# Rows of routed tokens fetched by indirect transfers and turned, instead of gathered with one-hot products

## The chip, the cores and the metric

The kernel is one program on one core of a Trainium2 chip. The metric is the device time of one execution in microseconds, the median of three runs. Other times come from one profiled execution.

## The reference

Two blocks of a model run one after the other on 512 tokens of 1024 elements, in float32. The first block has two mixing branches, then a hierarchical mixture of experts; the second has attention, a linear attention and a feed-forward part. Only the mixture of experts matters here:

```python
grp_logits = xt @ w_grp                                  # 4 groups
exp_logits = (xt @ w_exp).reshape(T, N_GROUPS, EXP_PER_GROUP)
sel_logits = take_along_axis(exp_logits, g_sel)          # the best group's 8 experts
top_l, top_e = lax.top_k(sel_logits, 2)                  # 2 experts for each token
...
def expert_block(args):
    xb, e = args
    return (jax.nn.silu(xb @ w1[e]) * (xb @ w3[e])) @ w2[e]
...
contrib = ybuf[dest] * w_s[:, None]
out = jax.ops.segment_sum(contrib, tok_s, num_segments=T)
```

There are 32 experts; `w1` and `w3` are 1024 x 512 and `w2` is 512 x 1024, 2 MiB each. 512 tokens with 2 experts each make 1024 rows.

## The kernel before

The experts are taken two at a time: 16 pairs, in 8 batches of two pairs. Each expert has 64 places (`SLOTS`), so that a pair fills the 128 partitions. A token's rank among those of its expert is its place. If an expert has more than 64 rows, further rounds follow (`r` is then not None); here the fullest expert has 55.

**Weights.** A ring of six buffers of 2 MiB (`ring[0]` to `ring[5]`) holds the weights of one pair: halves 0 and 1 are `w1`, 2 and 3 `w3`, 4 and 5 `w2`. SyncE (SP) loads half m of the next pair (L908) as soon as the products of this pair's half m are done (`half_used`). Pair 1's halves 0 and 1 have buffers of their own, `extra0` and `extra1` (L923, L926), so that the ring's halves 0 and 1 go to pair 2 at once.

**TensorE, in order, for each pair.** *up*: 64 products of the gathered rows `xgT` and the halves 0 to 3 (L3815). In odd pairs then the *gather* of the next batch (L3722): for 8 slices of 128 features, two parts of the rows (`xn_hi`, `xn_lo`) and 4 tiles of 128 tokens, one product of the rows with the one-hot table `sel`, 64 in all, with 256 columns each (the places of both pairs). Then the *turn* of `gated` (L3425), the *spread* of the pair before (16 products, L3761, added to `x` by VectorE), and *down*: 32 products with halves 4 and 5 (L3828).

**The other engines.** VectorE makes `sel` for the next batch with 16 comparisons and 16 comparisons with an add (`make_sel`, L2661, L2666), multiplies the gate (L2698), makes the one-hots of the spread (L2702), and adds the spreads to `x` (L2673). ScalarE copies the gathered banks into `xgT` (L1586) and the outputs out of PSUM (L1614). GpSimd has no work in this stage; its next instruction is a row scale of the stage after it (L1195).

**Before the experts.** The normalised rows `xn_at[1]` (tokens on partitions) are made by VectorE tile by tile (L2226), split into `xn_hi` and `xn_lo` (L2213), and turned for the router's logits. `pair(1)` gathers batch 1 and the first batches are written out; the batches 2 to 7 are gathered in a hardware loop (`pe.Fori(1, BATCHES - 1)`), `pair(m * 2 + 1)` gathering batch m + 1. After the experts come the end of the first block and all of the second.

Semaphores that the change touches: `sel_made` (one-hots ready), `rows_in` (four gathered banks of a batch written) and `rows_out` (a bank copied to `xgT`), `up_done` (a half's products done), `xn_lo_done` (a tile of `xn_lo` written).

Of the kernel before, what the change touches and what calls it, by code (L numbers as in the profile page):

```python
# [21 lines left out]
ALU = mybir.AluOpType  # L22
ACT = mybir.ActivationFunctionType
F32 = mybir.dt.float32
F32R = mybir.dt.float32r
I32 = mybir.dt.int32
# [3 lines left out]
P = 128  # L30
# [45 lines left out]
def two_blocks(nc, A, out):  # L76
    T, D = A["x"].shape[1:]
    NT, KT = T // P, D // P
# [17 lines left out]
    PAIRS = NE // 2  # L96
    ROUTED = NG + NE
    FAR = 4096
    FIRST_PLACE = -2 * ROUNDS * FAR
# [39 lines left out]


    gates_dram = nc.dram_tensor("branch_gates", [2 * KT, P, T], F32).ap()

    ctx = ExitStack()
    with ctx:
# [6 lines left out]
        def at(name, page, shape, dt=F32):  # L151
            return nc.alloc_sbuf_tensor_at(name, shape, dt, offset=base + int(page * PAGE))

        def sem(name):
            return ctx.enter_context(nc.semaphore(name))
# [46 lines left out]
        slot_gate, slot_token = slot_tables[:, 0, :], slot_tables[:, 1:1 + NT, :]  # L202
# [16 lines left out]
        w_lo = [at(f"w_lo{s}", 45 + 4 * s, [P, 4, 512], F32R) for s in range(2)]  # L219
        F = 53  # L220

        xn_at = {1: 41, 2: F + 36, 6: F + 40}
        xn_at = {n: at(f"xn_{n}", page, [P, NT, D]) for n, page in xn_at.items()}
        xn_at.update({n: xn_at[2] for n in (3, 4, 5)})
        gain = at("gain", F + 48, [P, D])
# [46 lines left out]

        EXTRA = 2
        extra = (at("extra0", 29, [P, 8, 512]), [at(f"extra1{q}", page, [P, 4, 512]) for q, page in enumerate((37, 49))])
        pair_both = at("pair_both", 16, [P, 2 * NT, 2, PAIRS])
        route_f = at("route_f", F + 50, [P, KT, ROUTED])
        routed_T = at("routed_T", 13, [P, KT, T])
# [161 lines left out]
        n_xn, n_tp, n_hi, n_lo = sem("n_xn"), sem("n_tp"), sem("n_hi"), sem("n_lo")  # L439
        first_by_dve, x_hi, x_lo = sem("first_by_dve"), sem("x_hi"), sem("x_lo")  # L440
        gain_in, gain_2_in, gain_4_in = sem("gain_in"), sem("gain_2_in"), sem("gain_4_in")
        const_pool, const_dve, params_in = sem("const_pool"), sem("const_dve"), sem("params_in")
# [3 lines left out]
        wsp_masked = sem("wsp_masked")  # L446
# [21 lines left out]
        xn_hi_done, xn_lo_done = sem("xn_hi_done"), sem("xn_lo_done")  # L468
# [3 lines left out]
        sel_made, selT_out = sem("sel_made"), sem("selT_out")  # L472

        rows_in, rows_out = sem("rows_in"), sem("rows_out")
        up_done, down_done = sem("up_done"), sem("down_done")
# [4 lines left out]
        extra_in = sem("extra_in")  # L480
# [28 lines left out]

        b_added = gates_stored  # L510
        quo_summed, quo_out = first_in[1], first_in[2]
        row_highs, row_lows = far_in
        rows_again = first_in[3]
        out_stored = sem("out_stored")

        block = ctx.enter_context(nc.Block())
# [13 lines left out]
        def rows_count(n, t):  # L530

            return n * NT + t + 1
# [239 lines left out]
            return i if r is None else i + r * PAIRS  # L772

        BATCHES = PAIRS // 2

        def batch_number(m, r):

            return m if r is None else m + r * BATCHES

# [4 lines left out]
        def gather_bank(b, first):  # L784

            return ((mb[0], mb[1], gb[2], gb[3]) if first else (mb[0], mb[1], mb[0], mb[1]))[b]
# [16 lines left out]
        def _(sp):  # L803
# [98 lines left out]
            def half_of(m, pair):  # L902

                return A[("w1", "w3", "w2")[m // 2]][ds(pair * 2 + m % 2, 1)]
# [14 lines left out]
            sp.wait_ge(w_lo_done, split_count(g_out.chunk1 - 1))  # L919
            for m in range(3, 6):  # L920
                load_half(m, 0)
            extra_0 = extra[0][:, :, :].rearrange("p k n -> p (k n)")
            sp.dma_start(extra_0, half_of(0, 1).rearrange("o p q k n -> p (o q k n)")).then_inc(extra_in, 16)  # L923
            sp.wait_ge(pe_tiles, 4 * g_out.chunk1)
            for q in range(2):
                sp.dma_start(extra[1][q][:, :, :].rearrange("p k n -> p (k n)"),  # L926
                             half_of(1, 1)[:, :, q, :, :].rearrange("o p k n -> p (o k n)")).then_inc(extra_in, 16)


            for m in range(EXTRA):  # L930
# [177 lines left out]
        def _(pool):  # L1108
            own = Chain(pool, pool_own)
# [80 lines left out]
            own.settle()  # L1190
            pool.sem_inc(r_pool, 1)


            pool.wait_ge(n_sd, rows_count(2, NT - 1))
            own.did(pool.tensor_scalar(ssq[:, :], ssq[:, :], EPS, None, ALU.add))  # L1195
# [30 lines left out]
            for n in range(SB_STEPS):  # L1226
                t, s = n % NT, n % 2
# [964 lines left out]
        def _(dve):  # L2192
            own = Chain(dve, dve_own)
# [481 lines left out]
            def experts_dve(r):  # L2675
# [42 lines left out]
                def pair(i, first=False, following=None, turned_late=False):  # L2718
                    n = pair_number(i, r)
                    if following is not None:  # L2720
                        make_sel(following, batch_number(following, r))
                    gate_up_product(n)
                    if not turned_late:
                        gatedT_copy(n)
                    if first:
                        dve.wait_ge(tabled, 1 if r is None else r + 1)
                        dve.tensor_copy(slot_tables[:, 0:2, :], gb[1][:, 0:2 * PAIRS]  # L2727
                                        .rearrange("p (v i) -> p v i", i=PAIRS)).then_inc(valued, 1)
                        dve.wait_ge(valued, 1 if r is None else r * NT + 1)
                        for t in range(1, NT):  # L2730
                            dve.tensor_scalar(slot_token[:, t, :], slot_token[:, 0, :], -float(t * P), None, ALU.add)\
                                .then_inc(valued, 1)
                        dve.wait_ge(valued, NT if r is None else r * NT + NT)
                    else:

                        if not isinstance(n, int) or n > 1:
                            dve.wait_ge(moe_added, n * 8 - 8)
                        for u in range(2 * NT):
                            if u == 3 and turned_late:
                                gatedT_copy(n)  # L2740
                            add_spread(n - 1, u, u // 2, u % 2, spread_bank(u))
                    make_selT(i)
                    outputs_low(i, n)
# [26 lines left out]

                pair(0, first=True, following=1)
                pair(1)
                with dve.Fori(1, BATCHES - 1) as m:
                    pair(m * 2, following=m + 1, turned_late=True)
                    pair(m * 2 + 1)
                pair(PAIRS - 2, turned_late=True)
                last_pair()
# [233 lines left out]
            for n in range(SB_STEPS):  # L3011
                h, t = divmod(n, NT)
# [364 lines left out]
        def _(pe):  # L3377
# [46 lines left out]
            def turn(dst, src, rows=P):  # L3424
                return pe.transpose(dst, src, ident[0:rows, 0:rows])  # L3425
# [290 lines left out]
            def experts_pe(r):  # L3716
# [28 lines left out]
                def gather(b):  # L3745

                    pe.wait_ge(sel_made, b * 16 + 16)
                    for k in range(KT):
# [5 lines left out]
                        if k % 2:  # L3754
                            ins.then_inc(rows_in, 1)

                def spread(n, t, half, bank):

                    half = slice(half * 512, (half + 1) * 512)
                    for part in (y_hi_sb, y_lo_sb):  # L3760
                        ins = pe.matmul(bank[:, :], selT[:, t * P:(t + 1) * P], part[:, half],  # L3761
                                        start=(part is y_hi_sb), stop=(part is y_lo_sb))
                    ins.then_inc(spread_done, 1)
# [65 lines left out]
                                     ring[4 + k // 2][:, 4 * q + 2 * (k % 2) + nh, :], start=(k == 0),  # L3829
                                     stop=(k == 3), skip_group_check=True)  # L3830

                def pair(i, first=False, ahead=False, odd=0, following=None):
                    n = pair_number(i, r)
                    up(i, first, ahead, odd)
                    if first:
                        gate_table()
                    if following is not None:
                        gather(batch_number(following, r))
                    if first or odd:
                        turn_gated(n)  # L3840
                    if first:
                        pe.wait_ge(valued, 1 if r is None else r * NT + 1)
                    else:
                        output_cut(n - 1)
                        for u in range(2 * NT):
                            if odd and u in (3, 4):
                                pe.wait_ge(rows_out, n * 2 + (u + 2))
                            elif u == 5 and not odd:
                                turn_gated(n)
                            elif u == 7:  # L3850
                                pe.wait_ge(moe_added, n * 8 + (3 - 8))
                            spread(n - 1, u // 2, u % 2, spread_bank(u))
                        pe.wait_ge(moe_added, n * 8 - 6)
                    pe.wait_ge(gatedT_out, n + 1)
                    for kh in range(2):
                        half_in(n, 4 + kh, ahead)
                        for k in (2 * kh, 2 * kh + 1):
                            for nh in range(2):
                                for q in range(2):
                                    ins = down_matmul(n, k, nh, q)  # L3860
                                if k == 3:
                                    ins.then_inc(down_done, 1)
                        if kh == 0:
                            ins.then_inc(down_done, 1)
# [40 lines left out]
                pair(1, ahead=r is None, odd=1, following=1)  # L3905
                with pe.Fori(1, BATCHES - 1) as m:
                    pair(m * 2)
                    pair(m * 2 + 1, odd=1, following=m + 1)
                pair(PAIRS - 2)
                last_pair()  # L3910

# [152 lines left out]
            for n in range(SB_STEPS):  # L4064
                h, t = divmod(n, NT)
# [255 lines left out]
```

## Time and profile before

| | us |
|---|---|
| median of 3 runs | 1666.09 |
| lowest, highest | 1663.88, 1666.44 |
| span of the profiled execution | 1661.6 |
| experts' stage in it | about 346 to 809 |

The span goes from the first to the last instruction. The profiled execution's own time outside its span is not given apart; the median of the runs is 4.5 us above the span. TensorE's granted clock is at its full level nearly all the time (mean 0.999). Matmuls are pipelined, so the duration of one is longer than its distance to the next; distances are read from the chain in order of time. The profile has two views of the transfers: stretches with the busy share of the 16 DMA engines and GB/s, and for each line that issues them the time from issue to landing.

### The profile page before, as it was taken

Reading aid. Unit: us, or ns where it says so; the run is one execution under the profiler, and the core shown is the slowest. Engines: PE = TensorE matmul, PEld = TensorE weight load, DVE = VectorE, ACT = ScalarE, POOL = GpSimd, SP = SyncE. Lnnn points to the kernel's source line nnn. Section 1 sums busy time; section 2 is a strip of 40 time slices with the busy share of each in tenths; the row PEclk is TensorE's granted clock in tenths of the full one; section 3 lists DMA queues with packets and bytes.
Section 4 is the critical chain, followed back from the end, with each engine's and each line's share of the span. In section 5 each row is a group of like instructions: output and inputs, shape, how many; then the busy total and the mean of one; then the engine's idle time right before and its main releaser. Section 6 shows DMA issues by size and latency. Waiting matters only on the chain.

```text
span 1661.6 us, 25424 instructions
## 1 busy us (share of the span) xinstructions
PE 1649.0 (99%) x10378; PEld 1246.5 (75%) x10378; DVE 1042.9 (63%) x1371; ACT 715.6 (43%) x906; POOL 109.6 (7%) x168
## 2 busy tenths in 40 slices
PE   9999999999999999999999999999999999999998
PEld 7899998864535545453688877788888889889986
DVE  6989777453243334323668746567675577878887
ACT  6576552411101101111456533344642367757775
POOL 4000100000000000000011022210000001000000
PEclk9999999999999999999999999999999999999999
DMA  7232224958999999999441232123353249667864
GB/s 279 66 114 76 102 81 183 400 208 341 427 428 429 429 428 429 427 429 428 185 177 33 100 102 77 51 77 129 114 179 110 92 146 255 158 182 226 202 144 121
DMA packets 92209, 355.65 MB, mean 214 GB/s; under 512 B 7936, under 2 KB 7952, under 8 KB 79824
## 3 DMA queue, kind: packets, MB, share of 16 engines
q1 hardware_dynamic: 79776, 328.04, 50.8%
q0 software_dynamic: 12336, 26.23, 8.0%
q8 instruction: 71, 1.16, 0.3%
q14 instruction: 26, 0.21, 0.0%
HBM read 347.97 MB, written 6.29 MB: 213 GB/s over the span
## 4 chain that ended last, share of the span: by engine, by line
PE 97%; DVE 1%; DMA 1%; ACT 1%; issue 0%; POOL 0%; ACTq 0%; POOLq 0%; DVEq 0%
PE bank L3400 33%; PE bank L3815 13%; PE bank L4267 9%; PE bank L3563 9%; PE bank L3828 7%; PE bank L4242 6%; PE bank L3722 4%; PE bank L3761 4%; PE bank L3998 2%; PE bank L3425 2%; PE bank L3446 1%; DMA stage<-in_w_ff 1%; PE bank L3923 1%; PE bank L4028 1%; PE bank L4051 1%; PE bank L4098 1%
## 5 line engine op out<-in xcount | busy, mean ns | idle before, releaser
L3815 PE MATMUL bank<-ring,xgT 128*64 128x512 f32 x992 | 216.1, 592 | 0.6 <-ACT xgT L1586 0.6
L3400 PE MATMUL bank<-act_hi,w_hi 128*128 128x512 f32 x544 | 215.3, 396 | 0.0
L3400 PE MATMUL bank<-act_hi,w_lo 128*128 128x512 f32 x544 | 212.0, 390 | 0.0
L3400 PE MATMUL bank<-act_lo,w_hi 128*128 128x512 f32 x544 | 211.8, 389 | 0.0
L3815 PEld LDWEIGHTS bank<-ring,xgT 128*64 128x64 f32 x992 | 71.8, 137 | 141.0 <-issue 140.0
L2198 DVE TENSOR_TENSOR w_lo<-w_stage,w_hi 128x2048 fp32r<-128x2048 f32 x51 | 116.9, 2292 | 66.6 <-ACT w_hi L1291 64.9
L1291 ACT ACTIVATE w_hi<-w_stage 128x2048 fp32r<-128x2048 f32 x50 | 96.0, 1921 | 144.8 <-PE bank L3400 133.4
L4267 PE MATMUL bank<-down,part_hi 128*128 128x512 f32 x448 | 138.2, 390 | 0.2 <-issue 0.2
L3400 PEld LDWEIGHTS bank<-act_hi,w_hi 128*128 128x128 f32 x544 | 102.2, 188 | 23.2 <-issue 2.8
L3400 PEld LDWEIGHTS bank<-act_hi,w_lo 128*128 128x128 f32 x544 | 102.1, 188 | 21.7
L1614 ACT ACTIVATE y_hi_sb<-bank,slot_tables 128x512 fp32r<-128x512 f32 x32 | 22.0, 687 | 222.0 <-PE bank L3828 220.7
L3400 PEld LDWEIGHTS bank<-act_lo,w_hi 128*128 128x128 f32 x544 | 102.2, 188 | 20.3
L3828 PE MATMUL bank<-ring,gatedT 128*64 128x512 f32 x512 | 113.4, 595 | 0.9 <-DVE slot_tables L2727 0.9
L2698 DVE TENSOR_TENSOR gated<-gated,bank 128x512 f32<-128x512 f32 x16 | 11.0, 688 | 161.6 <-PE bank L3815 161.6
L4267 PEld LDWEIGHTS bank<-down,part_hi 128*128 128x128 f32 x448 | 83.8, 188 | 18.3 <-issue 1.0
L3828 PEld LDWEIGHTS bank<-ring,gatedT 128*64 128x64 f32 x512 | 35.3, 137 | 70.5 <-issue 66.8
L4267 PE MATMUL bank<-down,part_lo 128*128 128x512 f32 x224 | 87.2, 389 | 0.0
L2673 DVE TENSOR_TENSOR x_tm<-x_tm,bank 128x512 f32<-128x512 f32 x128 | 78.5, 679 | 0.3 <-PE bank L3761 0.3
L2714 DVE SCALAR_TENSOR_TENSOR y_lo_sb<-bank,slot_tables,y_hi_sb 128x512 fp32r<-128x512 f32 x32 | 23.5, 750 | 70.2 <-ACT y_hi_sb L1614 69.9
L4242 PE MATMUL bank<-act_hi,slot_hi 128*128 128x256 f32 x224 | 63.5, 283 | 0.1
L3563 PE MATMUL bank<-row_hi,slot_hi 128*128 128x256 f32 x224 | 63.5, 284 | 0.0
L4242 PE MATMUL bank<-act_lo,slot_hi 128*128 128x256 f32 x224 | 63.4, 283 | 0.0
(587 smaller groups left out, 3778.8 us busy)
## 6 DMA issues: line engine op xcount, KB each, us to landing
ring<-in_w SPq DMA_DIRECT2D x93, 2048.0 KB, 16.3
w_stage<-in_w_in SPq DMA_DIRECT2D x39, 1024.0 KB, 5.0
w_stage<-in_w_ff SPq DMA_DIRECT2D x19, 1024.0 KB, 5.8
b_sum<-in_w_ff POOLq DMA_DIRECT2D x12, 1024.0 KB, 12.0
w_stage<-in_w_out SPq DMA_DIRECT2D x8, 1024.0 KB, 5.0
b_one<-in_w_ff SPq DMA_DIRECT2D x6, 1024.0 KB, 7.5
stage<-in_w_ff SPq DMA_DIRECT2D x5, 1024.0 KB, 6.2
x_tm<-in_x SPq DMA_DIRECT2D x8, 512.0 KB, 9.3
```

Source lines behind the costliest of these rows:

```text
L1291: act.activation(w_hi[s][:, 0:ktiles, :], w_stage[s][:, 0:ktiles, :], ACT.Copy)\
L2198: dve.tensor_tensor(w_lo[s][:, 0:ktiles, :], w_stage[s][:, 0:ktiles, :], w_hi[s][:, 0:ktiles, :].bitcast(F32), ALU.subtract).then_inc(w_lo ...
L2673: dve.tensor_tensor(xt, xt, bank[:, :], ALU.add).then_inc(moe_added, 1)
L3400: ins = pe.matmul(banks[j][:, :], left, right, start=(kc == 0 and k == 0 and n_pass == 0), stop=(kc == g.chunks - 1 and k == g.ktiles - 1 ...
L3425: return pe.transpose(dst, src, ident[0:rows, 0:rows])
L3563: ins = pe.matmul(bank_of[:, 256 * f:256 * f + 256], left[:, k, cols], right[:, k, :], start=(n in (0, 1, 3) and f == 0 and k == 0 and n_p ...
L3722: return pe.matmul(bank[:, (k % 2) * 2 * P:(k % 2 + 1) * 2 * P], part[:, t, k * P:(k + 1) * P], sel[:, t, :], start=start, stop=(part is x ...
L3761: ins = pe.matmul(bank[:, :], selT[:, t * P:(t + 1) * P], part[:, half], start=(part is y_hi_sb), stop=(part is y_lo_sb))
L3815: ins = pe.matmul(dst[mine, :], xgT[:, 4 * kh + k, slots], up_weights(2 * w + kh, q, k, ahead), start=(kh == 0 and k == 0), stop=(kh == 1 ...
L3828: return pe.matmul(gb[1 + nh][mine, :], gatedT[:, k, mine], ring[4 + k // 2][:, 4 * q + 2 * (k % 2) + nh, :], start=(k == 0), stop=(k == 3 ...
L4242: ins = pe.matmul(bank[:, 256 * f:256 * f + 256], left[:, k, cols], right[:, k, :], start=(n in (0, 1, 3) and f == 0 and k == 0 and n_pass ...
L4267: ins = pe.matmul(part_bank[h][n][j][:, :], left[:, ka, cols], right[:, k, :], start=(part_first[n] and kc == 0 and k == 0 and n_pass == 0 ...
```

## The change

The rows `xn_at[1]` are stored to a DRAM tensor `routed_rows`. For batches 2 to 7 (`FETCHED = 2`) GpSimd clears a buffer `slot_rows` and issues two indirect transfers per batch, one for each pair, that fetch the row of each place by its token number (`slot_row`; a place without a token has a number beyond the bound and is skipped). TensorE turns these rows, 16 turns of 128 x 128, into the banks that the one-hot products filled before. Batches 0 and 1 stay as they are. VectorE no longer makes `sel` for batches 2 to 7. The buffer `xn_at[1]` lies on other pages, and the load of `extra0`, which shares these pages now, is issued after the rows are stored and `xn_lo` is made.

```diff
-        xn_at = {1: 41, 2: F + 36, 6: F + 40}
+        xn_at = {1: 29, 2: F + 36, 6: F + 40}
+        slot_row = at("slot_row", 15, [P, PAIRS], I32)
+        slot_rows = at("slot_rows", 37, [P, 2, D])
...
 @ SyncE
-            extra_0 = extra[0][:, :, :].rearrange("p k n -> p (k n)")
-            sp.dma_start(extra_0, half_of(0, 1).rearrange("o p q k n -> p (o q k n)")).then_inc(extra_in, 16)
             sp.wait_ge(pe_tiles, 4 * g_out.chunk1)
             for q in range(2):
                 sp.dma_start(extra[1][q][:, :, :].rearrange("p k n -> p (k n)"),
                              half_of(1, 1)[:, :, q, :, :].rearrange("o p k n -> p (o k n)")).then_inc(extra_in, 16)
+            for t in range(NT):
+                sp.wait_ge(n_xn, rows_count(1, t))
+                sp.dma_start(rows_dram[t * P:(t + 1) * P, :], xn_at[1][:, t, :]).then_inc(rows_stored, 16)
+            sp.wait_ge(xn_lo_done, NT)
+            sp.wait_ge(rows_stored, STORED)
+            sp.dma_start(extra[0][:, :, :].rearrange("p k n -> p (k n)"),
+                         half_of(0, 1).rearrange("o p q k n -> p (o q k n)")).then_inc(extra_in, 16)
 @ GpSimd
+            pool.wait_ge(rows_stored, STORED)
+            pool.wait_ge(row_listed, LISTED)
+            pool.wait_ge(up_done, 4 + EXTRA)
+            for b in range(FETCHED, BATCHES):
+                if b > FETCHED:
+                    pool.wait_ge(rows_in, 4 * b)
+                own.did(pool.memset(slot_rows[:, :, :], 0.0))
+                own.settle()
+                for q in range(2):
+                    i = 2 * b + q
+                    pool.indirect_dma_start(slot_rows[:, q, :], None, rows_dram[:, :],
+                                            bass.IndirectOffsetOnAxis(ap=slot_row[:, i:i + 1], axis=0),
+                                            bounds_check=T - 1, oob_is_err=False).then_inc(rows_fetched, 16)
 @ VectorE
+                        if r is None:
+                            dve.tensor_scalar(slot_row[:, :], slot_token[:, 0, :], -float(FIRST_PLACE), None, ALU.add)\
+                                .then_inc(row_listed, 1)
...
-                    pair(m * 2, following=m + 1, turned_late=True)
+                    pair(m * 2, following=None if r is None else m + 1, turned_late=True)
 @ TensorE
+                def turn_slots(m):
+
+                    b = batch_number(m, r)
+                    pe.wait_ge(rows_fetched, m * 32 + (NONE_FETCHED - 32 * (FETCHED - 1)))
+                    for k in range(KT):
+                        if k in (4, 6):
+                            pe.wait_ge(rows_out, b * 4 + (k // 2 - 1))
+                        for q in range(2):
+                            first = (k % 2) * 2 * P + q * P
+                            ins = turn(gather_bank(k // 2, False)[:, first:first + P],
+                                       slot_rows[:, q, k * P:(k + 1) * P])
+                        if k % 2:
+                            ins.then_inc(rows_in, 1)
...
-                    if following is not None:
+                    if fetched:
+                        turn_slots(following)
+                    elif following is not None:
                         gather(batch_number(following, r))
...
-                    pair(m * 2 + 1, odd=1, following=m + 1)
+                    pair(m * 2 + 1, odd=1, following=m + 1, fetched=r is None)
```

## Rows read from the trace of the kernel before

**Rows 1.** The page: busy time by engine, and the last chain by engine.
```profile
PE 1649.0 (99%) x10378; PEld 1246.5 (75%) x10378; DVE 1042.9 (63%) x1371; ACT 715.6 (43%) x906; POOL 109.6 (7%) x168
...
PE 97%; DVE 1%; DMA 1%; ACT 1%; issue 0%; POOL 0%; ACTq 0%; POOLq 0%; DVEq 0%
```

**Rows 2.** Chain in order of time: start us, us, what; 360 to 860.
```profile
375.68 13.73 PE bank L3815 x64
...
433.46 13.73 PE bank L3815 x64
447.19 7.87 PE bank L3722 x64
455.06 0.44 PE bank L3425 x4
...
491.26 13.73 PE bank L3815 x64
...
790.56 0.03 issue
790.59 3.65 PE bank L3815 x16
```

**Rows 3.** Stretches: length; busy us by engine; TensorE's clock, DMA share, GB/s.
```profile
400.00:405.00 5.00, 5.00 (x24) 2.12 (x25) 3.99 (x10) 0.00 (x0) 0.00 (x0) 1.00 0.00 0
433.50:491.30 57.80, 57.80 (x298) 27.97 (x296) 20.66 (x48) 6.33 (x11) 0.00 (x0) 1.00 1.01 428
722.50:780.30 57.80, 57.80 (x298) 27.97 (x296) 16.89 (x33) 6.33 (x10) 0.00 (x0) 1.00 1.01 428
365.00:370.00 5.00, 4.12 (x30) 2.76 (x30) 2.68 (x10) 0.00 (x0) 0.00 (x0) 1.00 1.01 433
780.00:800.00 20.00, 19.97 (x94) 8.31 (x92) 10.31 (x14) 4.34 (x6) 0.00 (x0) 1.00 1.01 410
335.00:350.00 15.00, 14.04 (x109) 11.76 (x108) 13.76 (x57) 1.40 (x4) 0.00 (x0) 1.00 0.01 3
```

**Rows 4.** Ring loads by issue time, with us to landing; then TensorE's wait.
```profile
L908 SPq DMA_DIRECT2D ring<-in_w x1: 333/333/333, 433.5 to 433.5; - x1
DMA to landing us min/median/max: 14.4/14.4/14.4
...
L908 SPq DMA_DIRECT2D ring<-in_w x1: 333/333/333, 722.5 to 722.5; - x1
DMA to landing us min/median/max: 19.1/19.1/19.1
...
L908 SPq DMA_DIRECT2D ring<-in_w x1: 328/328/328, 768.9 to 768.9; - x1
DMA to landing us min/median/max: 21.6/21.6/21.6
...
PEld bank L3815 <- DMA ring<-in_w: 0.9, 1, 0.9
```

**Rows 5.** Single lines: ns min/median/max, first and last start.
```profile
L1586 ACT ACTIVATE xgT<-bank x28: 597/597/597, 391.5 to 744.1; 128x512 f32<-128x512 f32 x28
...
L1177 POOL MEMSET attT<- x1: 1813/1813/1813, 172.0 to 172.0; 128x2048 f32 x1
```

**Rows 6.** Timelines of SyncE's queue and of VectorE: start us, us.
```profile
350.53 25.52 SPq L908 DMA_DIRECT2D ring<-in_w  x6
382.58 0.33 SPq L937 DMA_DIRECT2D pT<-in_p  x1
...
337.78 1.22 DVE L2213 TENSOR_TENSOR xn_lo<-xn,xn_hi 128x1024 fp32r<-128x1024 f32 x1
```

**Rows 7.** Queues: packets, MB, share of 16 engines; 1050 to 1250, then whole span.
```profile
q0 software_dynamic: 1280, 4.20, 5.4%
...
q1 hardware_dynamic: 79776, 328.04, 50.8%
q0 software_dynamic: 12336, 26.23, 8.0%
```

More of the change, by code:

```diff
@@ L141, in two_blocks @@
     gates_dram = nc.dram_tensor("branch_gates", [2 * KT, P, T], F32).ap()
+    rows_dram = nc.dram_tensor("routed_rows", [T, D], F32).ap()
     ctx = ExitStack()
@@ L511, in two_blocks @@
         quo_summed, quo_out = first_in[1], first_in[2]
+        row_listed, LISTED = wsp_masked, 2
+        rows_fetched, NONE_FETCHED = params_in, 16 * 9
         row_highs, row_lows = far_in
         rows_again = first_in[3]
+        rows_stored, STORED = rows_again, 16 + 2 * 16 * NT
         out_stored = sem("out_stored")
@@ L774, in two_blocks @@
         BATCHES = PAIRS // 2
+        FETCHED = 2
         def batch_number(m, r):
@@ L2772, in experts_dve @@
                 pair(1)
+                if r is None:
+                    dve.wait_ge(sel_made, 16 * FETCHED)
+                    dve.sem_inc(sel_made, 16 * (BATCHES - FETCHED))
                 with dve.Fori(1, BATCHES - 1) as m:
-                    pair(m * 2, following=m + 1, turned_late=True)
+                    pair(m * 2, following=None if r is None else m + 1, turned_late=True)
                     pair(m * 2 + 1)
@@ L3830, in down_matmul, with pair @@
                                      stop=(k == 3), skip_group_check=True)
-                def pair(i, first=False, ahead=False, odd=0, following=None):
+                def pair(i, first=False, ahead=False, odd=0, following=None, fetched=False):
                     n = pair_number(i, r)
```

## The prediction

> **What bounds the kernel now.** I read the page first. TensorE is busy 99% of the span and 97% of the chain that ended last [rows 1], so a cut of TensorE work looks like a cut of the time. The share is an average over stages, so I went to the experts' stage: first to the chain of waits in order of time [rows 2]. There, one batch of two expert pairs repeats every 57.80 us (433.46 to 491.26) without a gap: an up product of 13.73 us, the gather of 7.87 us, a turn of 0.44 us, eight spreads, the down product, then the second pair without a gather. The reader is to see that TensorE paces this stage and that the edited gather is in its pace.
>
> The table of stretches gives the other half [rows 3]: in the same 57.80 us the DMA engines are 1.01 busy and move 428 GB/s, and still are in 722.5 to 780.3. One batch of pairs needs 12 loads of 2 MiB, 25.17 MB, and at 428 GB/s these take 58.8 us. The DMA engines are asked for one microsecond more per batch than TensorE allows. The loads' own rows confirm it [rows 4]: the load issued at 433.5 lands 14.4 us later, the same load of the batch five periods on, issued at 722.5 (289.0 us later), after 19.1 us. The lag grew 4.7 us in 5 periods, 0.94 us each, so 12 loads take 57.80 + 0.94 = 58.74 us. What hides this is the lead that the ring had at the start. It is used up at the very end: the load issued at 768.9 lands at 790.5, and the chain shows TensorE at 790.56 with 0.03 us between two pieces just there [rows 2]; the waits list has one wait of 0.9 us of TensorE's weight loads for a ring load, the only one [rows 4]. So the two limits meet at 790.5. The stream of loads is unbroken back to the empty stretch 400 to 405 [rows 3].
>
> **The change, part by part.** *TensorE.* Six gathers (batches 2 to 7) of 7.87 us go [rows 2]. In place of 64 products come 16 turns. Four turns of `gated` take 0.44 us, so 16 take 1.8 us; turns 9 and 13 wait for ScalarE to empty a bank, 0.60 us a piece [rows 5]: 0.44 us for the first four, then four evacuations of which two must be done before the last four turns, with some 0.2 us of handing over, make about 2.3 us. Bounds: 1.8 and, one evacuation after another, 4 us. TensorE saves 5.6 us per batch, 33 us in six (23 to 36). A batch then costs it 52.2 us of work.
>
> That saving can't be cashed. After the change the DMA engines still need 58.74 us for the loads of each batch, and no load becomes smaller or goes away. A faster TensorE frees ring buffers earlier, but the queue has not been empty since 405, so an earlier issue only waits longer. The last ring loads land when all bytes ahead of them have been moved; the last up product, spreads, down product and everything after follow from that landing by the same TensorE work as before. TensorE's 33 us turn into waits for ring loads. From this part the end moves by 0 us.
>
> *The added traffic.* Each of the six batches has two fetches of up to 128 rows of 4 KB. Places beyond an expert's rows hold an index beyond the bound and are to be skipped. Counted with the reference's routing on its inputs, 1024 rows are spread over 32 experts, 21 to 55 each; batch 2 has 109, batches 3 to 7 have 119, 104, 106, 167 and 155, together 651. The first fetch waits for the second half of pair 1, which `pT` waits for too (issued at 382.6) [rows 6]; it falls ahead of the idle 400 to 405 [rows 3], and its 109 rows (0.45 MB, 1.0 us) are absorbed there. The other five wait for the batch before to be turned, the first after about 450, and all run inside the unbroken stream. 651 x 4096 bytes are 2.67 MB: 6.2 us at the stream's 428 GB/s, 6.5 us at the 410 GB/s of 780 to 800 where smaller transfers are mixed in [rows 3]. They displace ring loads byte for byte, so the end moves by that.
>
> Is a fetched row as cheap as a byte of the ring? No row of before shows an indirect transfer. Nearest are the direct transfers from GpSimd's queue: the gate stores, 4.20 MB for 5.4% of 16 engines over 200 us, 389 GB/s while busy; the page's other queue has 328.04 MB for 50.8% of 1661.6 us, 389 GB/s too; all of GpSimd's traffic, mostly accumulating, 26.23 MB for 8.0%, 197 GB/s [rows 7]. So a plain transfer costs alike from both queues, and at the worst row 651 rows would take 13.5 us. Were empty places moved as well, 5 x 256 rows are 5.24 MB, 12.2 us at 428 and 26.6 us at 197. A second unknown is how rows are divided among the engines: experts fill only the first half of their places, and if that left half of the engines idle, the loaded ones would need twice as long, 13 us. Below, an even split gives 6.2. I take 8 us: nearest to the even split, a little above it because experts with 55 and 47 rows of 64 cannot split evenly and ten more transfers bring their completions. Could it be below nothing? Only if a second queue raised the total rate; that is a rival.
>
> The Trainium skill (DMA: Bandwidth & Descriptors, The descriptor swizzle) gives a map in which the first 32 places of each 64 lie on eight engines, four each. By it the most loaded engine would carry 52 of the rows and the delay would be 8.0 us as an estimate; no row here shows the map.
>
> *The store and the moved load.* Four stores of 512 KB and the load of `extra0` now come after the halves of `extra1`. The same 2 MB of `extra0` left the stretch before 335, and 2 MB of stores took its place. DMA engines are idle (0.01) from 335 to 350 [rows 3]. The load now also waits for the last `xn_lo` (337.8 + 1.2 = 339.0) [rows 6] and needs 4.9 us for its bytes and at most as much again on idle engines: landed by 349, read by pair 1 from 375.7 [rows 2], cost 0. What it delays on SP's queue is the first reload of the ring, issued at 350.5 [rows 6]: 11 us in hand, cost 0 (0 to 2; were the stores' completions late by 10 us, the idle 400 to 405 would take it up).
>
> *VectorE* loses the one-hots of six batches, 20.66 - 16.89 = 3.8 us a batch; it is busy 20.66 of 57.80 us, so 0 [rows 3]. *ScalarE* copies the same banks: 0. *GpSimd* is idle there; a clear of `slot_rows` is the size of one that took 1.81 us [rows 5]; behind its waits stands only the row scale of the next stage. A fetch must be in place a batch later, about 50 us; with clear, two issues, a queue of 16 to 25 us it needs some 30. Cost 0. `xn_at[1]` on other pages changes no wait.
>
> Sum: 0 + 8 + 0 = 8 us. The profiled span is 1661.6 us, so 1669.6; the median of the three runs is 1666.1, 4.5 us more (what lies around the span), so 1674.
>
> **Rivals.** (a) *Added bytes on a saturated stream, as above*: +8, range +5 to +14; chance 0.80. (b) *The other side: TensorE's saving is cashed.* The mechanism would be that 428 GB/s is what the one queue reaches and not what the engines can; rows fetched by another queue then ride beside it, and faster release lets more through. Single stretches reach 433 [rows 3]. It decides from the point where 390 us of stream shrink by 3.3 us more than the fetches cost, that is 10 us, 439 GB/s. Fully cashed it gives 1666.1 - 33 = 1633. Against it: 1.01 busy and a growing lag at any depth of the queue. Chance 0.07, mostly near 1660. The Trainium skill (DMA: Bandwidth & Descriptors, Issuing engines are not separate DMA queues) says that transfers of all issuing engines run on the same 16; by that the second queue adds nothing. (c) *Dear rows*: accumulating price or empty places moved: +13 to +27, 1680 to 1692; 0.05. (d) *A fetch comes late*: GpSimd needs more than 50 us per batch. At 60 us, TensorE waits 10 us in each of five batches, 1716; 0.02. (e) *The clock falls*: TensorE now waits. Its waits are short, since a load lands every 4.9 us and a half takes 3.43 us (a quarter of 13.73), and with 4.12 of 5 us busy it kept 1.00 in 365 to 370 [rows 3]. At 1.2 GHz a half would take 6.9 us and a batch over 100, some +40 us each; 0.01. The Trainium skill (TensorE: Matmul & The Clock Gate, HAM oscillation) tells of a kernel whose waits for data brought the half clock back each time; by it this would be the outcome if the waits were longer than its bursts. (f) *Nothing*: hidden or halved cost, below 3.3 us; 0.05.
>
> **From these to the numbers.** A change of 0.2% (3.3 us) is about what these runs can tell from none. Slower: (a), (c), (d), (e), 0.88; allowing for a mistake in the reading I give 0.85. Same 0.06. Faster 0.09. The predicted time is that of (a), 1674. The range holds (a) whole, 1671 to 1680, and reaches to the side of (f) and the start of (c): 1667 to 1682.
>
> **What the profile after would show.** If right: no pieces of the gather's line in the loop, turns instead; the same 428 GB/s and 1.01; TensorE no longer 99% busy but waiting for ring loads by name, 35 to 45 us in all; ring loads' lag level at 20 to 27 us (four to five loads in the queue), not growing; GpSimd's queue up by 3.1 MB; the last pair's half 3 landing about 8 us later than 790.5; `extra0` issued near 339. Wrong if the throughput rises above 435 GB/s, if TensorE waits for `slot_rows`, or if that half lands earlier than 790.5.

## The result and the profile after

The changed kernel takes 1673.36 us (median of 4 runs, 1671.48 to 1674.12), the kernel before 1666.17 (4 runs): a ratio of 1.0044 with a 95% interval of 1.0031 to 1.0056, which is 5 to 9 us. It is slower by 7.2 us; the forecast was 8 us and 1674.

The lines of the profile's page for the changed kernel: span, busy time, transfer queues, the last chain, and GpSimd's transfers.

```profile
span 1671.4 us, 24640 instructions
...
PE 1621.7 (97%) x10090; PEld 1209.9 (72%) x10090; DVE 1020.0 (61%) x1276; ACT 714.9 (43%) x906; POOL 133.0 (8%) x186
...
q1 hardware_dynamic: 80352, 330.14, 51.2%
q0 software_dynamic: 14064, 29.35, 8.5%
...
PE 81%; DMA 17%; DVE 1%; ACT 0%; issue 0%; SPq 0%; DVEq 0%; ACTq 0%
```

TensorE is busy 27 us less than in [rows 1], and yet the span is longer: 17% of the chain is now transfers of the ring. GpSimd's queue moves 3.12 MB more than in [rows 7], the 760 rows of the six batches.

These are stretches of the changed kernel, with the columns of [rows 3]:

```profile
335.00:350.00 15.00, 14.04 (x109) 12.00 (x110) 13.74 (x57) 1.40 (x4) 0.00 (x0) 1.00 0.63 244
395.00:400.00 5.00, 5.00 (x35) 4.62 (x35) 2.02 (x4) 1.20 (x2) 0.00 (x0) 1.00 0.98 412
400.00:405.00 5.00, 5.00 (x24) 2.19 (x24) 4.24 (x10) 0.00 (x0) 0.00 (x0) 1.00 0.06 20
405.00:410.00 5.00, 5.00 (x26) 1.72 (x24) 1.27 (x2) 1.37 (x2) 0.00 (x0) 1.00 0.80 279
433.50:491.30 57.80, 57.55 (x276) 23.83 (x274) 18.28 (x34) 7.06 (x12) 3.81 (x3) 1.00 1.01 427
450.00:780.00 330.00, 298.11 (x1387) 123.08 (x1387) 98.13 (x186) 33.07 (x55) 18.98 (x15) 1.00 1.01 427
```

From 450 to 780 the throughput is what it was (427 GB/s, 1.01 busy; 428 before), with another kind of bytes in it. TensorE stands still for 32 of 330 us, at full clock. The chain in order of time says for what; it is to be read against [rows 2].

```profile
408.62 13.73 PE bank L3862 x64
...
773.38 0.02 issue
773.40 25.62 DMA ring<-in_w
799.02 0.04 issue
799.06 3.65 PE bank L3862 x16
802.72 2.52 PE bank L3808 x10
```

Where the one-hot kernel ran on without a gap, the chain now goes through the load of the last pair's half 3: issued at 773.4, landed 25.6 us later, at 799.0. The same half landed at 790.5 before. To take out what varies between profiles ahead of the stage, I use one measure from here on: from the start of pair 2's up product to the start of the last pair's products with half 3. It is 790.59 - 408.37 = 382.2 us before (408.37 is the start of that piece in its chain) and 799.06 - 408.62 = 390.4 after: 8.2 us more. Each value comes from one profile; where two runs should agree, they do within 0.2 us (e1 and the kernel before, e2 and the changed kernel, e6 and e7 below).

The fetches by their line, with the time from issue to landing:

```profile
L1217 POOL DMA_INDIRECT slot_rows<-routed_rows,slot_row x12: 997/1002/1123, 385.6 to 689.3; - x12
DMA to landing us min/median/max: 10.3/12.8/15.4
```

The queues in 450 to 780, where all fetches of batches 3 to 7 lie (packets, MB, share of the engines):

```profile
q1 hardware_dynamic: 9501, 138.32, 98.6%
q0 software_dynamic: 1440, 2.67, 2.1%
```

2.67 MB are the 651 counted rows exactly; rows beyond the bound are not moved. A fetch is in place 15 us after its issue. The fetch of batch 3, issued at 452.5 and 453.8, is turned from about 502 on, 33 us after it landed; later batches have some 38 us.

### The profile page after: what moved, and what is told of

Its sections match the earlier page's. It is cut to its first block, busy times and chain, and to the rows that moved or that the text cites. A ratio compares the mean times of both kernels' runs of the same rounds, so it can differ in the third digit from the quotient of the medians.

```text
span 1671.4 us, 24640 instructions
## 1 busy us (share of the span) xinstructions
PE 1621.7 (97%) x10090; PEld 1209.9 (72%) x10090; DVE 1020.0 (61%) x1276; ACT 714.9 (43%) x906; POOL 133.0 (8%) x186
## 4 chain that ended last, share of the span: by engine, by line
PE 81%; DMA 17%; DVE 1%; ACT 0%; issue 0%; SPq 0%; DVEq 0%; ACTq 0%
PE bank L3433 33%; DMA ring<-in_w 17%; PE bank L4316 9%; PE bank L3596 8%; PE bank L4291 8%; PE bank L3862 7%; PE bank L4047 2%; PE bank L3875 2%; PE bank L3458 2%; PE bank L3479 1%; PE bank L3808 1%; PE bank L3755 1%; PE bank L4077 1%; PE bank L4100 1%; PE bank L4147 1%; PE bank L3972 1%
## 5 line engine op out<-in xcount | busy, mean ns | idle before, releaser
L3862 PE MATMUL bank<-ring,xgT 128*64 128x512 f32 x992 | 222.7, 595 | 34.9 <-DMA ring<-in_w 34.3
## 6 DMA issues: line engine op xcount, KB each, us to landing
b_sum<-in_w_ff POOLq DMA_DIRECT2D x12, 1024.0 KB, 10.9
```

Source lines behind the costliest of these rows:

```text
L3862: ins = pe.matmul(dst[mine, :], xgT[:, 4 * kh + k, slots], up_weights(2 * w + kh, q, k, ahead), start=(kh == 0 and k == 0), stop=(kh == 1 ...
```

## The experiments

The ratio of each run is taken to runs of the kernel before on the same chip. "Late" is the measure above less 382.2 us. The diffs show the main lines of each edit, "..." marks what is left out, and comments in them are mine.

| run | us (median) | ratio to before (interval) | measure, us | late, us |
|---|---|---|---|---|
| changed kernel | 1673.36 | 1.0044 (1.0031 to 1.0056) | 390.4 | 8.2 |
| e1 no transfers | 1666.29 | 1.0003 (0.9994 to 1.0012) | 382.2 | 0.0 |
| e2 one-hot gathers, fetches beside them | 1673.67 | 1.0046 (1.0032 to 1.0059) | 390.3 | 8.1 |
| e3 two more buffers | 1672.50 | 1.0041 (1.0027 to 1.0054) | see the text | |
| e4 all rows skipped | 1667.26 | 1.0008 (0.9999 to 1.0017) | 383.1 | 0.9 |
| e5 places 0 to 31 | 1671.91 | 1.0038 (1.0025 to 1.0052) | 388.7 | 6.5 |
| e6 places 0 to 63 | 1679.15 | 1.0079 (1.0065 to 1.0092) | 394.9 | 12.7 |
| e7 all places | 1679.56 | 1.0082 (1.0068 to 1.0096) | 394.8 | 12.5 |
| e8 before, light loads | 1665.29 | 0.9996 (0.9986 to 1.0005) | | |
| e9 changed, light loads | 1633.20 | 0.9804 (0.9788 to 0.9821) | | |
| e10 two more buffers, order of use | 1671.65 | 1.0031 (1.0019 to 1.0044) | 386.1 | 3.9 |
| e11 eight buffers in turn | 1667.82 | 1.0013 (1.0004 to 1.0022) | 383.5 | 1.3 |
| e12 eight buffers, no transfers | 1661.39 | 0.9967 (0.9958 to 0.9977) | 376.7 | -5.6 |

**Is it the fetches?** e1 takes the transfers away and leaves everything else; e4 issues them and moves nothing; e2 does them beside the old gathers.

```diff
 @ e1
-                    pool.indirect_dma_start(slot_rows[:, q, :], ...).then_inc(rows_fetched, 16)
+                    pool.sem_inc(row_listed, 1)
...
-                    pe.wait_ge(rows_fetched, m * 32 + (NONE_FETCHED - 32 * (FETCHED - 1)))
+                    pe.wait_ge(row_listed, m * 2 + (LISTED - 2 * (FETCHED - 1)))
 @ e2
-                    pair(m * 2, following=None if r is None else m + 1, turned_late=True)
+                    pair(m * 2, following=m + 1, turned_late=True)
...
-                    pair(m * 2 + 1, odd=1, following=m + 1, fetched=r is None)
+                    pair(m * 2 + 1, odd=1, following=m + 1)
```

> The changed kernel without its twelve indirect transfers: GpSimd clears the buffer and signals, TensorE turns the cleared rows, the store and the moved load stay. It leaves out the routed rows of batches 2 to 7. Theory of the stream (the DMA engines set the end, TensorE's saving is worth nothing, the fetches are the whole loss): 1666, within 1.5 us of the kernel before, TensorE waiting 30 to 37 us for ring loads. Rival that TensorE's saving is cashed once the fetches are gone: about 1633. Rival that the loss comes from the store, the moved load or the turns: stays near 1673.

> The changed kernel with its fetches, but the rows of batches 2 to 7 gathered with one-hot products as before; the fetched rows are not used. Nothing of the output is left out. Theory of the stream: as slow as the changed kernel, 1673 to 1674, because the loads and fetches of a batch need about 60 us and the one-hot kernel's TensorE 57.8 us. Rival that TensorE's waits for fetched and turned rows make the loss: 1666. Rival that both limits add up: above 1680.

> The changed kernel with a list in which every row number lies beyond the bound (1024 and up): twelve indirect transfers are issued and move no row. It leaves out the routed rows of batches 2 to 7. If a skipped row costs nothing and a transfer nearly nothing: as without transfers, 1666 to 1667. If the 8.3 us by which the last half landed later hold 2 us for ten transfers beside 6.2 us for 651 rows: 1668. If skipped rows cost as much as fetched ones: 1674 or more.

e1 came out as the kernel before in both the time (1.0003) and the measure (382.2): the fetches are the whole loss, and 33 us less TensorE work are worth nothing. TensorE's freed time is there as waits for loads, at a throughput of 428 GB/s. The next lines are e1's two sums of that kind in the waits list of 440 to 830 (us in total, times, longest), and its queue in 450 to 780:

```profile
PEld bank L3860 <- DMA ring<-in_w: 38.5, 24, 2.1
PE bank L3860 <- DMA ring<-in_w: 27.2, 26, 1.3
```

```profile
q1 hardware_dynamic: 9693, 141.25, 100.6%
```

e2 is the mirror of it: all of TensorE's old work and the fetches are as slow as the changed kernel (8.1 us late), so what TensorE saves does not matter on this side either. e4 is 0.9 us late: ten transfers that move nothing cost the stream 0.1 us each by the measure; the medians alone (1.0008, interval from 0.9999) do not tell that from nothing. A finer reading supports it: from one wait for a load to the next one, six loads later, 29.4 us pass in e1's chain, and 29.5 to 29.6 in e4's where two transfers lie between.

**Does TensorE's saving exist?** In e8 (the kernel before) and e9 (the changed kernel) the loads of pairs 3 to 14 bring half the bytes.

```diff
-                    load_half(m, i + 1)
+                    sp.dma_start(ring[m][:, 0:4, :].rearrange("p k n -> p (k n)"),
+                                 half_of(m, i + 1)[:, :, 0, :, :].rearrange("o p k n -> p (o k n)")).then_inc(ring_in[m], 16)
```

> The kernel before with half of the bytes in the loads of pairs 3 to 14: only the first expert's half of each buffer is loaded; it leaves out the second expert's weights there. TensorE's work is the same. Theory: TensorE paced this kernel to the edge, so 1666 (0 to 1 us less). If hidden waits for loads cost it more: well below.

> The changed kernel with the same loads of half the bytes for pairs 3 to 14; it leaves out the second expert's weights there. Theory: with the stream out of the way TensorE's saving of about 5.6 us in each of six batches shows: 1633, 33 us under the kernel before with light loads. Rival that the turns cost as much as the gathers, or that TensorE waits for the fetched rows: near 1666.

It does: 1665.29 - 1633.20 = 32.1 us. The one-hot kernel does not gain from lighter loads (0.9996), so TensorE paced it all through the stage. In e9's chain one batch takes 485.80 - 433.46 = 52.3 us, in place of 57.8:

```profile
433.46 13.73 PE bank L3863 x64
447.19 0.60 PE bank L3459 x4
447.79 0.02 issue
447.81 0.61 ACT xgT L1614
448.42 0.04 issue
448.46 1.58 PE bank L3459 x12
450.05 3.66 PE bank L3809 x16
...
485.80 13.73 PE bank L3863 x64
```

Between up product and spreads lie 2.86 us: the 16 turns, the turn of `gated`, and one wait for ScalarE (four of the turns run during that wait and so are not in the chain). Before there were 7.87 + 0.44 us [rows 2].

**What does a row cost?** In e5 to e7 the list of rows is 0 to 127 and the bound cuts it, so that places 0 to 31, 0 to 63 or all are filled in each of the ten transfers.

```diff
+            own.did(pool.iota(slot_row[:, :], pattern=[[0, PAIRS]], base=0, channel_multiplier=1))
+            own.settle()
...
-                                            bounds_check=T - 1, oob_is_err=False).then_inc(rows_fetched, 16)
+                                            bounds_check=31, oob_is_err=False).then_inc(rows_fetched, 16)     # 63, 127; e4: base=1024, bound 511
```

> The changed kernel with row number p for place p and the bound at 31: each indirect transfer fetches 32 rows, to places 0 to 31; ten transfers in the stream, 320 rows, 1.31 MB. It leaves out the routed rows of batches 2 to 7. 4096 bytes at a sixteenth of 428 GB/s take 0.153 us. Rows dealt evenly over 16 engines: 3.1 us over the kernel without transfers (1669). The first 32 places on eight engines, four each: 6.1 us (1672). Eight neighbouring places to one engine: four engines carry all, 12.2 us (1678).

> As the run with 32, bound at 63: 64 rows to places 0 to 63, 640 rows in the stream, 2.62 MB, nearly the bytes of the true lists. It leaves out the routed rows of batches 2 to 7. Even: 6.1 us (1672), as the changed kernel or a little less. Half of the engines carry eight rows each: 12.2 us (1678), clearly over the changed kernel with the same bytes.

> As the run with 32, bound at 127: all 128 places, 1280 rows in the stream, 5.24 MB. It leaves out the routed rows of batches 2 to 7. By bytes 12.2 us (1678) in every theory of the split; if the most loaded engine counts it equals the run with 64 rows, if bytes count it is 6.1 us over it. A cost per transfer would come on top in all three.

The queue of the transfers in 450 to 780 (packets, MB, share), one line each for e5, e6 and e7:

```profile
q0 software_dynamic: 1440, 1.32, 1.2%
```

```profile
q0 software_dynamic: 1440, 2.62, 2.1%
```

```profile
q0 software_dynamic: 1440, 5.24, 3.9%
```

The bytes double from run to run; the delay goes 6.5, 12.7, 12.5 us. Bytes in total do not decide. 64 rows in places 0 to 63 cost as much as 128 rows in all places, and the first 32 cost half of that. That fits a split in which places 0 to 63 lie on half of the engines, and 0 to 31 on the same half with four rows each. A row of 4096 bytes takes 0.153 us at a sixteenth of 428 GB/s, an estimate, which gives 6.1 and 12.2 us. The runs rule out rows dealt evenly (3.1 and 6.1) and eight neighbouring places to an engine (12.2 for the first 32); another split with the same largest load would fit as well. The Trainium skill (DMA: Bandwidth & Descriptors, The descriptor swizzle) gives this split for a plain transfer to 128 partitions. These three runs agree with it for the indirect one.

The changed kernel's own trace shows the same with the true lists. These are the pieces of its chain that are waits for loads, from 532 to 711; each load waited for is six loads after the one of the line above:

```profile
532.86 25.63 DMA ring<-in_w
562.22 26.99 DMA ring<-in_w
592.96 25.62 DMA ring<-in_w
622.32 27.58 DMA ring<-in_w
653.64 25.64 DMA ring<-in_w
683.01 27.90 DMA ring<-in_w
```

Start and length added give the landings: 558.5, 589.2, 618.6, 649.9, 679.3, 710.9. Six loads take 29.4 us where no fetch lies between, and 30.7, 31.3 and 31.6 us with the fetches of batches 5, 6 and 7. These fetches cost 1.4, 2.0 and 2.3 us. Batch 7 has fewer rows than batch 6 (155 against 167) and costs more. By the split above the reference's routing puts 8, 13 and 16 rows on the most loaded engine in them, 1.2, 2.0 and 2.4 us as an estimate; by bytes, batch 7 would be the cheaper one of the two (1.5 against 1.6 us).

**Where else could time come from?** The DMA engines idle between 395 and 410 (the stretches above: 0.1 + 4.7 + 1.0 = 5.8 us), because the pages for further loads are missing. From 398 on the split rows (`xn_hi`, `xn_lo`) are not needed any more. e3 puts their pages to use as two more buffers, for halves 0 and 1 of odd pairs from pair 3 on; e10 is e3 with the loads issued in the order of use; e11 uses all eight buffers in turn; e12 is e11 without the transfers.

```diff
 @ e3
+        wide = [at(f"wide{m}", page, [P, 8, 512]) for m, page in enumerate((21, 41))]
...
+                        half_used(j * 2 + odd, m)
+                        if m < 2:
+                            load_next(m, j * 2 + (odd + 2), odd)     # pair after next, ring or wide by parity
 @ e10: load_next(0) and load_next(1) behind half 5 of the next pair
 @ e11
+        eight = ring[0:4] + wide + ring[4:6]
...
+            with sp.Fori(0, 3) as j:
+                for s in range(6, 30):
+                    n, m = j * 4 + (s // 6 + 2), s % 6
+                    slot_used(n, m)      # the buffer's load of eight loads ago
+                    load_slot(s, n)      # into eight[s % 8]
```

> The changed kernel with two more ring buffers for halves 0 and 1, on the pages of the split rows, which are free after batch 1 is gathered: pair 3's halves are loaded at about 397 in place of 412, and from there even and odd pairs have buffers of their own. Further rounds (none is run with these inputs) are not provided for. Theory of the stream: the DMA engines' idle time between 398 and 406, about 7 us, is filled, so the whole stream ends 7 us earlier: 1666. If the stream is not what sets the end from 406 on, but bursts of the fetches that single waits feel: 1673, or between.

> The kernel with two more ring buffers again, but in the loop the loads of halves 0 and 1 of the pair after next are issued behind the next pair's half 5, so that loads stand in the queue in the order of their use. Further rounds are not provided for. If the run without this order gained only 0.9 us because two early halves stood ahead of the ones needed sooner: the idle time left is some 3 us less than in the changed kernel, so 1670. If filling the idle time is worth nothing: 1673.

> The changed kernel with a ring of eight buffers used in turn, in the order of use, from pair 2's half 4 on (the six buffers and the pages of the split rows). Further rounds are not provided for. The changed kernel's DMA engines are idle for 5.8 us between 395 and 410; theory of the stream: all of it is filled, every later load lands that much earlier, 1667.5. If the end is not set by the stream: 1673. Below 1666 would need more than the idle time gives.

> The ring of eight buffers without the indirect transfers (the cleared rows are turned). It leaves out the routed rows of batches 2 to 7, and further rounds. Theory of the stream: both effects add, 1666 - 5.8 - 0, 1660; here TensorE's saving lets the filled idle time show below the kernel before. If the one-hot kernel's time were a floor of TensorE or of something else: 1666.

e3's forecast missed: it was 1666, and 1672.5 were measured. Its DMA engines are busy through the empty stretch, as meant. The same table shows something else: at three places, of which the lower rows show one, TensorE's clock fell to half for a few us after a wait.

```profile
400.00:410.00 10.00, 10.00 (x47) 4.31 (x47) 5.62 (x13) 1.13 (x2) 0.00 (x0) 1.00 1.02 428
...
554.00:556.00 2.00, 1.28 (x6) 0.14 (x2) 0.00 (x0) 0.60 (x1) 0.00 (x0) 1.00 1.04 442
556.00:558.00 2.00, 0.11 (x2) 0.11 (x4) 0.00 (x0) 0.00 (x0) 0.00 (x0) 1.00 0.96 410
558.00:560.00 2.00, 2.00 (x6) 0.59 (x8) 0.00 (x0) 0.00 (x0) 0.00 (x0) 0.51 1.02 434
560.00:562.00 2.00, 2.00 (x8) 0.62 (x6) 0.00 (x0) 0.00 (x0) 0.00 (x0) 0.64 0.98 418
```

TensorE stood for 2.6 us (0.72 + 1.89) and then took 5.38 us for a piece with one half that takes 3.68 otherwise. The three losses of 1.7 us add up to nearly what e3 lacks, so they are a rival explanation. The landings in e3's chain answer it: 30.7 us pass from 557.9 to 588.6, across the first loss, as in the changed kernel with its full clock (558.5 to 589.2), and 29.4 us from 649.3 to 678.7, across the second (29.4 from 649.9 to 679.3). So these two losses are hidden behind the stream. The third lies where TensorE's waits move on to another half and cannot be compared like this. The chain at the end shows where the gain went:

```profile
748.31 25.63 DMA ring<-in_w
773.94 0.04 issue
773.98 3.65 PE bank L3883 x16
777.64 2.50 PE bank L3824 x10
...
781.98 7.02 PE bank L3896 x32
789.00 13.73 PE bank L3883 x64
802.73 2.50 PE bank L3824 x10
```

Halves 0 and 1 of the pair after next stood in the queue ahead of halves that were needed sooner. So the last half waited for is one of the pair before the last, landed at 773.94, with 28.8 us of TensorE work from it to the last pair's spreads at 802.73, against 802.72 in the changed kernel (from the start of pair 2's up product, at 409.42 and 408.62, it is 0.8 us less). The last pair's own up product (789.00, 13.73 us) runs without a wait: the end of the stream had stopped being what TensorE waits for. In order of use (e10, forecast 1670) the delay falls from 8.2 to 3.9 us by the measure. That profile is of the fastest of its six runs (1668.17). Four of the six lie at 1671.6 to 1672.2, and the median, 1671.65, is not clear of e3's by the intervals; so e10 shows the direction, not the size. e11 leaves 1.3 us of 8.2, and a time of 1667.82 (forecast 1667.5), 1.9 us over the kernel before. That is 6.9 us back by the measure where the idle time held 5.8; what the last 1.1 us are is open. Its stretches show the idle time filled:

```profile
395.00:400.00 5.00, 5.00 (x39) 4.78 (x38) 1.15 (x2) 1.36 (x3) 0.00 (x0) 1.00 1.00 421
400.00:405.00 5.00, 5.00 (x23) 2.60 (x23) 5.00 (x12) 0.00 (x0) 0.00 (x0) 1.00 1.00 419
405.00:410.00 5.00, 5.00 (x26) 1.72 (x24) 0.62 (x2) 1.07 (x2) 0.00 (x0) 1.00 1.02 436
```

e12 (1661.39, forecast 1660) is below the kernel before: filled idle time shows as soon as TensorE has time in hand and the fetches are gone. No run that computes the whole output is faster than the kernel before. Eight buffers with the one-hot gathers were not run; by e8, where the lighter loads gained nothing, I expect nothing from them.

## Why the prediction was right

- *The stream sets the end*: shown by e1 (nothing gained without fetches), e2 (nothing lost with the old gathers) and e12 (gained only by moving the stream forward). Two limits met in the kernel before; taking one away leaves the other. The forecast 58.74 us for the 12 loads of a batch are 2 x 29.4 = 58.7 us between the landings of e1.
- *TensorE saves 5.6 us a batch, 33 in all*: 5.5 a batch in e9's chain (57.8 - 52.3), 32.1 in all. Hidden until e9.
- *The fetches cost 8 us*: 8.2 by the measure, 7.2 in the medians, whose interval is 5 to 9. The size was in part luck. "They displace ring loads byte for byte" did not hold: e5 to e7 and the single batches go by the most loaded engine, and the even price of 6.2 us by bytes would have been too low. The 8 was a choice between 6.2 and 13 with a reason, uneven experts and the transfers' completions, that pointed the right way but gave no number. Worked out from the runs, the true lists put 52 rows on one engine, 8.0 us as an estimate; with e4's 0.9 us for ten transfers it is 8.9 at most, where 8.2 were seen.
- *Skipped rows are not moved*: the queue moved 2.67 MB, the bytes of the 651 rows, and 0.01 MB in e4. The accumulating queue's price (13.5 us) did not apply.
- *The store and the moved load cost 0*: e1, which keeps both, is as fast as the kernel before, but the reason given was not the whole one. The load of `extra0` waited for the stores to land, not for the last `xn_lo`: SyncE waited 10.9 us for `routed_rows`, the stores took 9.6 to 11.2 us. It was issued at 340.5, forecast 339.0, and landed in 7.8 us, before the first reload.
- *The lag is level at 20 to 27 us*: the loads' medians are 25.1 to 25.6 in each 50 us from 500 to 750, after 22.1 in 450 to 500; single loads up to 27.9. *TensorE waits 35 to 45 us*: 31.9 us idle in 450 to 780 and 3.6 in the 20 us after.
- *Rivals*: the cashed saving needed a higher throughput; it stayed at 427. No wait for fetched rows appears, and a fetch landed 10.3 to 15.4 us after its issue, sooner than the queue of 16 to 25 us that was allowed for it. The prediction took TensorE's waits as short; single ones reached 2.8 us. In the changed kernel the clock stayed full (1.00) through them. Other runs show that the clock rival was not empty: e3 lost the clock at three places, e6 at three and e10 at one.

## What to carry to other kernels

When an engine and the transfers are both near 100%, compute both demands for one round of the loop and follow the lag of a load over the rounds: a growing lag says that the transfers are the lower limit and only a lead hides it. Then work taken from the engine is worth nothing, and what is added to the transfers is paid in full; what pays is idle time of the transfers ahead of the stream, filled in the order of use. What e3 lacked against e11 is the order, as I read the chains; e10, the run made to test it, shows only the direction. A fetch of rows costs by its most loaded DMA engine, so where the rows land matters as much as how many they are.

## What the runs showed of the hardware

- An indirect transfer to 128 places does not cost by its bytes: filling the first 32 places delayed the stream 6.5 us over ten transfers, the first 64 12.7, all 128 12.5. In the changed kernel 155 rows cost 2.3 us and 167 rows 2.0.
- Ten indirect transfers that skip every row cost the stream 0.9 us. Each takes GpSimd 1.0 us to issue, whether it moves 0, 32, 64 or 128 rows (993 to 1123 ns in the changed kernel and e4 to e7).
- In e3 TensorE's clock fell to half (0.51) after the engine had stood for 2.6 us, and was full again from 562 on. In e6 it fell at three places and in e10 at one, each time after TensorE had stood for 1.9 to 2.1 us. The changed kernel, with 32 us of waits in 330 and stands of up to 1.9 us, and e7, with stands of up to 2.0 us, show no such place, so the length of the last stand alone does not tell the two cases apart.
- Mixed with rows of 4 KB from another queue the 16 engines moved 427 GB/s, as they did without (428).
